# Summing a token's two expert rows on the chip with one-hot float32 products, group by group, instead of through a table in memory

## The reference, cut to what matters

```
u = rmsnorm(h, ffn_norm)
h = h + hier_moe(u, ...)              # 64 experts in 8 groups of 8
return rmsnorm(h, final_norm)[:, N_META:]

def hier_moe(xf, ...):
    g_sel = argmax(xf @ w_group + b_group)            # one group for each token
    top_val, top_idx = top_k(e_in_group, 2)           # two experts, both of that group
    gate = p_sel * softmax(top_val)
    for each expert e:  y = (silu(x @ w1[e]) * (x @ w3[e])) @ w2[e]   # w1, w3: 1024 x 256, w2: 256 x 1024
    out[token] = sum over its two experts of gate * y
```

## Time and profile before

| what | value |
|---|---|
| median of 3 runs | 1469.39 us (1464.86 to 1470.57) |
| the profiled execution: time | 1471.87 us |
| the profiled execution: span, first to last instruction | 1470.2 us |
| mean granted clock of PE | 0.983 |
| PE busy | 1391.1 us, 95% |
| DVE, ACT, POOL busy | 712.4, 451.7, 99.7 us |
| moved by DMA | 303.12 MB, 206 GB/s in the mean |

### The profile page before, as it was taken

One profiled execution on the slowest core, in us unless ns is written; L12 is line 12 of the kernel. 1 busy time (PEld: TensorE's weight loads), 2 busy tenths in 40 slices (PEclk: granted clock), 3 DMA queues, 4 the chain that ended last, 5 costly groups with the idle time before them and its releaser, 6 DMA issues. The chain is left out here.

```text
span 1470.2 us, 21191 instructions
## 1 busy us (share of the span) xinstructions
PE 1391.1 (95%) x8531; PEld 990.9 (67%) x8531; DVE 712.4 (48%) x1515; ACT 451.7 (31%) x889; POOL 99.7 (7%) x132
## 2 busy tenths in 40 slices
PE   9999999999999999999989999999998788788887
PEld 8888888787888877677768888855554344344433
DVE  6555565433531154657758555444543433334336
ACT  6534355222322147545543456400000000000003
POOL 0000000000000000000000011211111111111100
PEclk9999999999999999999999999999999999999999
DMA  6111111112224335112136634899999999999986
GB/s 174 44 29 44 29 30 44 30 33 86 78 94 115 106 93 158 58 37 72 65 116 231 250 123 150 299 417 419 418 419 419 420 419 420 419 419 419 420 351 279
DMA packets 119796, 303.12 MB, mean 206 GB/s; under 512 B 30977, under 2 KB 77057, under 8 KB 94354
## 3 DMA queue, kind: packets, MB, share of 16 engines
q1 hardware_dynamic: 107666, 276.53, 50.1%
q0 software_dynamic: 12032, 25.22, 4.5%
HBM read 278.58 MB, written 37.78 MB: 215 GB/s over the span
## 5 line engine op out<-in xcount | busy, mean ns | idle before, releaser
L2449 PE MATMUL ps<-r,m_xT 128*64 128x256 f32 x2048 | 258.6, 406 | 54.0 <-DMA r<-in_w 53.4
L132 PE MATMUL ps<-uTh,h_wh 128*128 128x512 f32 (+2 forms) x672 | 255.7, 380 | 0.0
L134 PE MATMUL ps<-uTh,h_wl 128*128 128x512 f32 (+2 forms) x672 | 248.0, 369 | 0.0
L133 PE MATMUL ps<-uTl,h_wh 128*128 128x512 f32 (+2 forms) x672 | 247.9, 369 | 0.0
L2449 PEld LDWEIGHTS ps<-r,m_xT 128*64 128x64 f32 x2048 | 146.5, 140 | 147.7 <-DMA r<-in_w 60.4
L2299 ACT ACTIVATE m_sig<-ps,scale 128x128 f32<-128x128 f32 x64 | 23.5, 367 | 450.6 <-PE ps L2449 450.6
L132 PEld LDWEIGHTS ps<-uTh,h_wh 128*128 128x128 f32 x672 | 126.5, 188 | 22.4 <-issue 0.4
L134 PEld LDWEIGHTS ps<-uTh,h_wl 128*128 128x128 f32 x672 | 126.4, 188 | 18.7
L133 PEld LDWEIGHTS ps<-uTl,h_wh 128*128 128x128 f32 x672 | 126.7, 189 | 18.1 <-issue 0.2
L2352 DVE SCALAR_TENSOR_TENSOR m_prod<-ps,scale,m_sig 128x128 f32<-128x128 f32 x64 | 22.4, 351 | 230.2 <-ACT m_sig L2299 230.2
L2431 PE MATMUL ps<-r,m_hT 128*64 128x512 f32 x512 | 125.6, 612 | 2.3 <-DVE m_hT L2362 1.8
(11 more groups left out here) (374 smaller groups left out, 2084.7 us busy)
## 6 DMA issues: line engine op xcount, KB each, us to landing
r<-in_w SPq DMA_DIRECT2D x190, 1024.0 KB, 28.8
h_w<-in_w_in SPq DMA_DIRECT2D x37, 512.0 KB, 4.2
gates<-h_sg POOLq DMA_DIRECT2D x16, 512.0 KB, 2.9
r<-y_moe SPq DMA_DIRECT2D x8, 1024.0 KB, 11.8
br_gate<-gates SPq DMA_DIRECT2D x14, 512.0 KB, 5.0
e_wo<-in_w_out SPq DMA_DIRECT2D x4, 1024.0 KB, 7.6
f_x<-in_x SPq DMA_DIRECT2D x8, 512.0 KB, 5.4
h_half<-f_half SPq DMA_DIRECT2D x8, 512.0 KB, 3.2
```

What stands on the lines that cost most here:

```text
L132: pe.matmul(out, lh, rh, start=start, stop=False)
L133: pe.matmul(out, lh, rl, start=False, stop=False)
L134: return pe.matmul(out, ll, rh, start=False, stop=stop)
L2449: ins = pe.matmul(bank(UP_BANK + e % 2, 0, DE, CAP * f, CAP * (f + 1)).rearrange("p (r f) -> p r f", r=2), xT[i % 2][:, j, CAP * k:CAP * ( ...
```

## The change

No table `y_moe` is written and read any more (save in the path that isn't entered). A token's two rows are summed in PSUM while the experts run:

- Before the first expert, the tokens of each group are numbered (`ranks`), and lists are made of the tokens of each group with 192 places (`spots`, `lists`): `to_row` for places 0 to 127 and `to_half` for places 128 to 191. `row` and `spread_rows` lay out a group's list along the columns of PSUM, for each group anew.
- For each pair, DVE makes `hot`, 128 x 192: one where the token of a row is the token of a place in the group (`one_hot`). `results` writes y over x, in the same tile. PE then does `combine`: two products of 128 weight columns by 512 (places 0 to 127, both halves of the width), and two of 64 weight columns by 512 (places 128 to 191, one in each half of the array). They are plain float32, and add up in PSUM over the four pairs of a group.
- After each group, ACT squares the sums (`roots`; its main output goes to `o`, which is the fourth tile `x[3]`), DVE adds what belongs together (`sums`) and scales (`scaled`) into `o` and `o2`, and POOL scatters them to the output (`give`). Only when `o` is written out may POOL gather the next pair into that tile.
- The PSUM banks are laid out anew: up products of both parities share a bank, `turn` comes in two halves, the sums take banks 5 to 7.
- The end is gone: no load of the table, no additions, and no stores by SP but those of `give`.

```diff
+        hot = [sb(f"m_hot{b}", [P, GC]) for b in range(2)]
+        o, o2 = x[ROWBUF - 1], g.o2
...
+        UP_BANK, X_BANK, Y_BANK, H_BANK, SUM_BANK, MORE_BANK = 0, 1, 2, 4, 5, 7
+        x_bank = lambda i, q: Y_BANK + 1 if (i, q) == (0, 1) else X_BANK
...
+        PER = PER_GROUP // 2
...
-            def load_y(t):
-                if t % 2 == 0:
-                    sp.wait_ge(up_mm, EXPERTS - NBUF + 3 + t // 2)
-                sp.dma_start(pair[t], y_src[t * P:(t + 1) * P, :, :]).then_inc(pair_in[t], 16)
...
+            def give(n):
+                pool.wait_ge(to_ok, 3)
+                pool.wait_ge(o_ok, 3 * n + 3)
+                settle(pool, g)
+                pool.indirect_dma_start(out=g.out[0], out_offset=bass.IndirectOffsetOnAxis(ap=to_row[:, n:n + 1], axis=0),
+                                        in_=o, in_offset=None, bounds_check=SEQ - 1, oob_is_err=False).then_inc(o_out, 16)
+                pool.indirect_dma_start(out=g.out[0].rearrange("t (c d) -> (t c) d", c=2),
+                                        out_offset=bass.IndirectOffsetOnAxis(ap=to_half[:, n:n + 1], axis=0),
+                                        in_=o2[:, :], in_offset=None, bounds_check=2 * SEQ - 1, oob_is_err=False).then_inc(o2_out, 16)
...
+            for n in range(XB - 1, PAIRS):
+                if n == ROWBUF - 1:
+                    pool.wait_ge(rows_zero, 1)
+                elif n >= ROWBUF:
+                    pool.wait_ge(cmb_mm, n - ROWBUF + 1)
+                if n >= ROWBUF and n % ROWBUF == ROWBUF - 1:
+                    give(n // ROWBUF - 1)
+                    pool.wait_ge(o_out, 16 * (n // ROWBUF))
+                settle(pool, g)
+                pool.indirect_dma_start(out=x[n % ROWBUF], out_offset=None, in_=g.h,
+                                        in_offset=bass.IndirectOffsetOnAxis(ap=g.src[:, n:n + 1], axis=0),
+                                        bounds_check=SEQ - 1, oob_is_err=False).then_inc(x_in[n % ROWBUF], 16)
+            give(GROUPS - 1)
...
+            def roots(n):
+                act.wait_ge(cmb_mm, PER * (n + 1))
+                act.activation(o, g.ps[:, SUM_BANK * 512:SUM_BANK * 512 + D], ACT.Square, accum_out=st[:, 2:3]).then_inc(ss_ok, 1)
+                if n:
+                    act.wait_ge(o2_out, 16 * n)
+                act.activation(o2[:, :], bank(MORE_BANK), ACT.Square, accum_out=st[:, 0:1]).then_inc(ss_ok, 1)
+                act.wait_ge(s2_ok, 2 * n + 2)
+                act.wait_ge(ss_ok, 2 * n + 2)
+                act.activation(st[:, 4:6], st[:, 2:4], ACT.Sqrt, scale=1.0 / D, bias=g.eps[:, :]).then_inc(rt_ok, 1)
             act.wait_ge(g.rows_ok, 6)
+            act.activation(warm[:, :], g.eps[:, :], ACT.Sigmoid)
             for e in range(EXPERTS):
                 act.wait_ge(up_mm, e + 1)
-                act.activation(sig[e % 2][:, :], bank(UP_BANK + e % 2, 0, HALF), ACT.Sigmoid,
-                               scale=g.scale[:, e:e + 1]).then_inc(sig_ok, 1)
+                act.activation(sig[e % 2][:, :], up_out(e, 0, HALF), ACT.Sigmoid, scale=g.scale[:, e:e + 1]).then_inc(sig_ok, 1)
+                if e % PER_GROUP == 1 and e > PER_GROUP:
+                    roots(e // PER_GROUP - 1)
+                    act.activation(warm[:, :], g.eps[:, :], ACT.Sigmoid)
+            act.activation(warm[:, :], g.eps[:, :], ACT.Sqrt)
+            roots(GROUPS - 1)
...
+            def ranks():
+                dve.tensor_scalar(member, g.not8[:, :, :].rearrange("p t g -> p (t g)"), 0.0, None, ALU.is_equal).then_inc(member_ok, 1)
...
+                                  ALU.mult).then_inc(member_ok, 1)
+                dve.wait_ge(rank_mm, 1)
+                c.link(dve.tensor_tensor(ranked, member, rank_out, ALU.mult))
+                c.link(dve.tensor_reduce(out=in_group, in_=by_tile(ranked), axis=AX.X, op=ALU.add))
...
+            def one_hot(i):
+                dve.wait_ge(row_mm, i // PER + 1)
+                if i >= 2:
+                    dve.wait_ge(cmb_mm, i - 1)
+                dve.tensor_scalar(hot[i % 2][:, :], row_out, g.srcf[:, i:i + 1], None, ALU.is_equal).then_inc(hot_ok, 1)
+            def sums(n):
+                dve.wait_ge(ss_ok, 2 * n + 2)
+                dve.tensor_tensor(st[0:64, 3:4], st[0:64, 0:1], st[64:P, 0:1], ALU.add).then_inc(s2_ok, 1)
+                dve.tensor_tensor(st[64:P, 3:4], st[64:P, 0:1], st[0:64, 0:1], ALU.add).then_inc(s2_ok, 1)
+            def scaled(n):
+                dve.wait_ge(rt_ok, n + 1)
+                dve.reciprocal(st[:, 6:8], st[:, 4:6]).then_inc(rc_ok, 1)
+                if n == 0:
+                    dve.wait_ge(gain_in, 16)
+                dve.wait_ge(rc_ok, n + 1)
+                dve.scalar_tensor_tensor(out=o, in0=g.ps[:, SUM_BANK * 512:SUM_BANK * 512 + D], scalar=st[:, 6:7], in1=gain,
+                                         op0=ALU.mult, op1=ALU.mult).then_inc(o_ok, 1)
+                for q in range(2):
+                    rows = slice(64 * q, 64 * (q + 1))
+                    dve.scalar_tensor_tensor(out=o2[rows, :], in0=bank(MORE_BANK, 0, 512, 64 * q, 64 * (q + 1)), scalar=st[rows, 7:8],
+                                             in1=gain[rows, 512 * q:512 * (q + 1)], op0=ALU.mult, op1=ALU.mult).then_inc(o_ok, 1)
...
+                if e == 1:
+                    lists()
+                    most()
+                if e % PER_GROUP == 1:
+                    spread_rows(e // PER_GROUP)
+                if e % 2 == 0 and 2 <= e < EXPERTS - 2:
+                    one_hot(e // 2 - 1)
+                if e % PER_GROUP == 1 and e > PER_GROUP:
+                    sums(e // PER_GROUP - 1)
+                if e % PER_GROUP == 2 and e > PER_GROUP:
+                    scaled(e // PER_GROUP - 1)
+            one_hot(PAIRS - 1)
             results(EXPERTS - 1)
+            sums(GROUPS - 1)
+            scaled(GROUPS - 1)
...
+            def row(n):
+                pe.wait_ge(spread_ok, 2 * n + 2)
+                if n:
+                    pe.wait_ge(hot_ok, PER * n)
+                pe.matmul(row_out[:, 0:P], spread[:, 0, :], g.ident[:, :], start=True, stop=True)
+                pe.matmul(row_out[:, P:GC], spread[0:GC - P, 1, :], g.ident[0:GC - P, 0:GC - P], start=True, stop=True).then_inc(row_mm, 1)
+            def turn(i, q):
+                if q == 0:
+                    pe.wait_ge(x_in[i % ROWBUF], 16 * (i // ROWBUF) + 16)
                 settle(pe, g)
                 if i:
-                    pe.wait_ge(xT_ok, 2 * i)
-                for j in range(DK):
-                    ins = pe.transpose(bank(X_BANK + j // 4, j % 4 * P, P), x[i % ROWBUF][:, j::DK], g.ident[:, :])
-                    if i == 0 and j == DK // 2 - 1:
-                        ins.then_inc(x_half, 1)
+                    pe.wait_ge(xT_ok, 2 * i + q)
+                for j in range(4):
...
+            def combine(i):
+                first, last = i % PER == 0, i % PER == PER - 1
+                if first and i:
+                    pe.wait_ge(o_ok, 3 * (i // PER))
+                pe.wait_ge(hot_ok, i + 1)
+                for q in range(2):
+                    pe.wait_ge(y_ok, 4 * i + 3 + q)
+                    pe.matmul(bank(SUM_BANK + q), hot[i % 2][:, 0:P], x[i % ROWBUF][:, q * 512:(q + 1) * 512], start=first, stop=last)
+                for q in range(2):
+                    ins = pe.matmul(bank(MORE_BANK, 0, 512, 64 * q, 64 * (q + 1)), hot[i % 2][:, P:GC],
+                                    x[i % ROWBUF][:, q * 512:(q + 1) * 512], start=first, stop=last)
+                ins.then_inc(cmb_mm, 1)
+            ranks()
...
+                if e == EXPERTS - 1:
+                    combine(PAIRS - 2)
                 if e < EXPERTS:
...
+                if e == 1:
+                    lists(0)
+                if e % 2 == 1 and 3 <= e < EXPERTS - 1:
+                    combine((e - 3) // 2)
                 if e % 2 == 0 and e // 2 + 1 < PAIRS:
-                    turn(e // 2 + 1)
+                    turn(e // 2 + 1, 0)
                 if 1 <= e < EXPERTS - 2 or e == EXPERTS:
                     down(e - 1)
+                if e % 2 == 0 and e // 2 + 1 < PAIRS:
+                    turn(e // 2 + 1, 1)
+                if e % PER_GROUP == 2 and e < EXPERTS:
+                    row(e // PER_GROUP)
                 if e < EXPERTS:
                     pe.wait_ge(hid_ok, e + 1)
                     settle(pe, g)
-                    pe.transpose(bank(H_BANK + e % 2, 0, P), hid[:, :], g.ident[:, :]).then_inc(h_tr, 1)
+                    pe.transpose(h_out(e), hid[:, :], g.ident[:, :]).then_inc(h_tr, 1)
+                if e == 1:
+                    lists(4)
+            combine(PAIRS - 1)
...
-            def from_last(t, start):
-                for q in range(2):
-                    ins = pe.matmul(g.ps[:, added(t) + q * 512:added(t) + (q + 1) * 512], token[:, t * P:(t + 1) * P],
-                                    y[LAST % XB][:, q * 512:(q + 1) * 512], start=start, stop=not start)
```

(54 more changed lines are left out.)

307 lines of the change are left out of this document (143 added, 164 removed).

## The result

| what | before | after |
|---|---|---|
| median | 1467.12 us (1463.00 to 1470.57, 4 runs) | 1558.16 us (1557.00 to 1561.58, 4 runs) |
| ratio to before, 95% interval | | 1.0626 [1.0589, 1.0662] |
| profiled execution, span | 1470.2 us | 1557.3 us |
| mean granted clock of PE | 0.983 | 0.970 |
| first up product starts | 948.3 | 947.4 |

What follows compares the result with a forecast made beforehand. PE was taken to bound the changed kernel all the way: 1444.4 + 14 + 58.8 + 11.9 = 1529.1 us for the last up product, + 20 = 1549.1 span, less 0.8: 1548 us, 5.4% slower, range 1477 to 1595.

Steps and rivals of the forecast that it cites:

- PE alone, 1444.4: Expert loop: without waits, the last up product ends at 1444.4 us, from 1354.0 + 83.7 + 2.7 + 4.0.
- the group's end, 14: After each group: late sigmoid and scaling make PE wait 2.0 us, after seven groups 14 us.
- The stall, 58.8: Pairs 7, 11, 15 to 31: PE waits 8.4 us for a gather behind the scatter, seven times, 58.8 us.
- upper end: Scatter and gather landing in 9.5 and 11.5 us, with more rows per scatter: a stall of 14 to 15 us.
- the idle ends: Landings on idle queues: 3.4 us for a gather, 3.8 for the scatter, 7.2 together, no stall.
- the first rival (no stall): At the group's gather: it lands in time because queues are nearly empty; 1478 us, 0.6% slower, chance 0.12.
- The clock, 11.9: Behind each of seven stalls: 3.4 us at half speed costs PE 1.7 us, 11.9 us in all.
- The products as cover (second rival): Expert loop: combine products fit under PE's 73 us of cover, no gather late; 1454 us, 1.0% faster, chance 0.07.
- The pair scatters: Each pair's scatter goes, 64 rows of 4 KB beside 6 MB of weights, 4%; said not to help.
- The end, 20: From the last up product's end to the last instruction: 20 us against 43.0.

Runs made afterwards that it cites:

- Experiment 1: The changed kernel with the scaled sums in a tile of their own, so POOL's gather no longer waits for the scatter to land: 1528.62 us, ratio 1.0393.
- experiment 2: Experiment 1 with POOL issuing the gather ahead of the two scatters instead of behind them: 1481.31 us, ratio 1.0074 to the kernel before.
- experiment 6: Experiment 2 with results split into a high and a low fp32r part, eight products of 128 weight columns, seven w2 buffers: 1468.69 us, ratio 1.0002.
- 8: Experiment 6 with the scaling of a group's first 128 places issued one expert earlier, right behind `sums`: 1459.43 us, ratio 0.9920 to the kernel before.
- Experiment 4: The kernel before without its pair scatters to the table, the end reading as many bytes from `h_half`: 1448.66 us, ratio 0.9871.

## Why the prediction was right

The mechanism was the forecast's: PE becomes the bound, and once in a group it stands until a gather behind a scatter has landed. Experiment 1 takes out the wait for the scatter's landing, and experiment 2 the gather's place behind the scatters. Together the time falls by 76.9 us (81 by the ratios), where the prediction had 58.8 + 11.9 = 70.7 for stall and clock. By its own steps:

- **PE alone, 1444.4, and the group's end, 14.** The sum 1458.4, from a first up product at 948.3, is 510.1 us of loop. Experiment 2, which has no stall, runs from 940.4 to 1455.6: 515.2. So 5 too few, out of errors of both signs. A combine is 2.83 and not 2.7, and the halved turn adds to it: two up products a pair apart start 15.71 us apart in its steady state (1063.63 and 1079.34 in the kernel after), where 12.74 + 2.7 = 15.44 were forecast, 8 us too few in 31 pairs. The group's end was overrated:

```profile
1027.10 1.28 ACT L2311 ACT_TABLE_LOAD   x1
...
1029.69 0.30 ACT L2311 ACTIVATE m_stat<-m_stat,eps 128x2 f32<-128x2 f32 x1 [1.31 <-DVE m_stat L2413]
1030.01 1.28 ACT L2320 ACT_TABLE_LOAD   x1
...
1031.41 0.35 ACT L2317 ACTIVATE m_sig<-ps,scale 128x128 f32<-128x128 f32 x1
```

  The prediction let the table load for the root come behind the wait for `sums`, as the sigmoid's does in the earlier trace rows. Here it ran ahead of it (1027.10, DVE's sums ended at 1029.65), so the sigmoid of expert 10, whose up product ended at 1030.97, was 0.4 late and not 1.8, and PE's second half of the turn didn't wait. Only the 0.5 for the scaling is left: 3.2 us in all for the 14. The rest is small: `row` takes 0.67 and not 0.5, and the last two experts, whose down products come ahead of the up products and wait for DVE, some 5 us more than two in the steady state.
- **The stall, 58.8.** 62.3 measured. The size of one was too low, the number too high. Six stalls are 9.8 to 10.8 us, not 8.4: in the first of them the scatter landed in 9.9 and the gather in 7.5, 17.4 together, close to the 18.1 that the prediction had for full queues and not to the 15.5 it chose. Its reason, that the queues aren't deep any more, was true (a weight load lands in 8.4 us in the median of the page, 28.8 before). The gather did get faster (6.9 to 7.8 us at the six, 10.0 in the median before). The scatter got slower (8.9 to 10.4 us against 8.1), and it isn't the same scatter: the two scatters of a group move 0.45 to 0.60 MB, nearly all of it in the first, where 64 rows of 4 KB were 0.26 MB. The prediction named these rows only for its upper end. How much of the 9.9 us they make is open. For the seventh group the idle ends held:

```profile
1499.04 1.00 POOL L2257 DMA_INDIRECT out<-rows,m_to_row  x1 [28.78 <-DVE m_o L2425]
...
1503.23 1.03 POOL L2274 DMA_INDIRECT rows<-h_half,src  x1 [1.89 <-DMA out<-rows,m_to_row]
...
1507.09 0.69 PE L2536 MATMUL ps<-ident,rows 128*128 128x128 f32 x4 [0.24 <-DMA rows<-h_half,src]
```

  By then all weights are loaded (DMA share 0.06 from 1500 to 1538 us, above), the scatter lands in 3.3 and the gather in 3.7, and PE waits 0.24 us. The prediction had put the idle ends at 3.8 and 3.4. In this one group the first rival (no stall) is what happened. Stalls of 0 and of 10 us come from the same instructions in the same program; the two scatters move as many bytes here (0.49 MB) as at the other six, and what the trace has different is the weights beside them. The Trainium skill (DMA: Bandwidth & Descriptors, section Anatomy of one DMA) has about 2 us and the bytes over the bandwidth for such a DMA, an estimate of 3.2 us for 128 rows of 4 KB. The trace is near it in the seventh group (3.3 and 3.7 us), and in the other six it has two to three times as much.
- **The clock, 11.9.** The low stretches last 2.9 to 5.7 us behind the tile's arrival, 25.7 in all at half speed, so 12.8 us. That they come six times and not seven, and are longer than the 3.4 us taken, nearly cancels.
- **The products as cover (second rival).** Experiment 2 is this case with every late gather taken away, and it is 0.7% slower than before, not 1% faster. The 2.83 us of a combine decide it: with 2.04 (experiment 6) and the group's end cleared (8) the change does win, by 0.8%.
- **The pair scatters.** "It does not help" holds for the kernel after, where no weight is waited for. Experiment 4 shows that it is 19 us as soon as the transfers are the bound; the prediction had no number for it.
- **The end, 20.** 20.4 us against 43.0. The sum for the span was 1549.1, and it is 1557.3; 5.1 from loop and group's end, 3.5 from the stalls, 0.9 from the clock and 0.4 from the end are 9.9, less 0.9 for a start at 947.4 it is 9.0, for the 8.2 between the two. That the time came within 10 us is in part luck: the group's end was 11 us too high, the loop with `row` and the last experts some 15 too low, and seven stalls of 8.4 stand for six of 10.4. The steps and their order held; four of their sizes didn't.

Left open: how the landing grows with a DMA's own rows and with the bytes in flight beside it. The runs have the second at two states, with weights moving and without; nothing between was measured.

## What to carry to other kernels

A transfer that waits in an in-order queue behind an instruction that waits for something else is late by that wait, even if its own buffer has been free all along: issue first what the busiest engine will want next, and give an output a tile of its own. Price a dependent chain of small DMAs by landings measured beside the same traffic, not by those on idle queues; here that was 17 us against 7. And when an engine gets new work, look at who has to prepare it: issuing one scaling of DVE earlier was worth 9 to 12 us here, the cheaper products themselves 11 to 13.

## What the runs showed of the hardware

A scatter of up to 128 rows of 4 KB landed in 8.9 to 10.4 us while weights moved, and in 3.3 to 3.4 us without them. When far less stood in the weights' queue (their own loads landed in 8.4 us and not in 28.8), the gathers of one pair's rows landed sooner, in 7.8 us in the median instead of 10.0, but still not near the 3.7 us without weights. The DMA engines were full all the same in both (share 1.02 over 1105 to 1418 us before, 1.00 to 1.03 from 1040 to 1052 us after).

Each time that PE stood still for about 10 us its clock fell to the lower level, and stayed there for 3 to 6 us of new work; behind the stalls of 6.4 to 7.4 us of experiment 1 it was low too (0.50; the first down product took 3.68 us).

Four fp32r products of 128 weight columns by 512, half of the places of two of them zeros, took 1.13 us where the four plain float32 ones, two of them side by side in 64 columns, took 2.83, and eight took 2.04. A table load was seen ahead of the wait of the instruction it serves (L2311, with two waits ahead of it in the code), and behind it in another place (L2299, with one); whether the number of waits has to do with it wasn't tried.
